# The adaLN modulation of a two-layer encoder: 16 blocks as products on TensorE ahead of the first norm, 32 behind retention and the second layer's 48 in the MLP, as row sums over transposed weights

## What is computed

```python
mod = jax.nn.silu(c) @ w_ada + b_ada            # (1024) @ (1024, 6144), for 2 vectors c
sh1, sc1, g1, sh2, sc2, g2 = jnp.split(mod[:, None, :], 6, axis=-1)
h = _rmsnorm(x, norm1_g) * (1.0 + sc1) + sh1
mix, new_state = _token_mixers(h, ...)
x = x + g1 * (mix @ w_out)
h = _rmsnorm(x, norm2_g) * (1.0 + sc2) + sh2
x = x + g2 * (jnp.square(jax.nn.relu(h @ w_up)) @ w_down)
```

## Time and profile before

| | |
|---|---|
| median of 3 runs | 3626.52 us (3621.28 to 3632.74) |
| profiled execution | 3623.91 us |
| its span | 3622.1 us |
| PE busy | 3361.5 us, 93% |
| DVE busy | 1731.1 us, 48% |
| ACT busy | 950.7 us, 26% |
| POOL busy | 871.6 us, 24% |
| weight units, 512 KB each | 212, median 3.7 us from issue to landing |
| adaLN units, 384 KB each | 128, median 3.8 us |

### The profile page before, as it was taken

The page is one execution under the profiler, slowest core; times in us unless marked ns, Lnnn a source line. Parts: engine busy times, 40 slices in busy tenths (PEclk is TensorE's granted clock), DMA queues, the critical chain, the costliest instruction groups (busy, mean ns, idle before and its releaser), DMA issues.

```text
span 3622.1 us, 50742 instructions
## 1 busy us (share of the span) xinstructions
PE 3361.5 (93%) x19632; PEld 3031.9 (84%) x19632; DVE 1731.1 (48%) x2991; ACT 950.7 (26%) x1697; POOL 871.6 (24%) x478
## 2 busy tenths in 40 slices
PE   3499999899998999999998999998999999999998
PEld 2497889766777999999998878985667899999998
DVE  6833522365448554445565352325643833333335
ACT  2013111266343111111122231116644411111112
POOL 0121222222122232223223112231212222233231
PEclk7599999999998999999999999999999999999999
DMA  6521136723411222222212112565232111111111
GB/s 220 161 65 38 49 102 185 222 66 70 89 37 63 71 71 71 80 70 73 81 53 80 43 30 82 164 210 141 61 70 52 41 41 42 46 46 41 46 47 66
DMA packets 139878, 297.54 MB, mean 82 GB/s; under 512 B 52940, under 2 KB 73748, under 8 KB 138816
## 3 DMA queue, kind: packets, MB, share of 16 engines
q1 hardware_dynamic: 96912, 217.82, 21.4%
q10 hardware_dynamic: 42800, 77.46, 6.6%
HBM read 228.45 MB, written 53.56 MB: 78 GB/s over the span
## 4 chain that ended last, share of the span: by engine, by line
PE 74%; DVE 11%; issue 3%; ACTq 3%; DMA 3%; PEld 3%; ACT 2%; SPq 1%; POOL 0%; DVEq 0%; POOLq 0%; PEldq 0%
PE ps L1253 19%; PE ps L1228 13%; PE ps L1169 9%; PE ps L901 6%; PE ps L956 4%; DVE ada_acc L1792 4%; PE ps L1146 3%; PE ps L1039 3%; PE ps L1082 2%; PE ps L1102 2%; PE ps L883 2%; PE ps L736 2%; PE ps L925 1%; DVE tn L1862 1%; DVE act_lo L2221 1%
## 5 line engine op out<-in xcount | busy, mean ns | idle before, releaser
L658 POOL CAST w_hi<-raw 128x1024 fp32r<-128x1024 f32 x212 | 231.8, 1093 | 2261.0 <-PEq L1259 534.8
L2039 DVE SCALAR_TENSOR_TENSOR x<-ps,mod,x 128x352 f32<-128x352 f32 (+2 forms) x768 | 352.7, 489 | 516.5 <-PE ps L1253 426.5
L661 POOL TENSOR_TENSOR w_lo<-raw,w_hi 128x1024 fp32r<-128x1024 f32 x212 | 522.0, 2462 | 36.7 <-POOL w_hi L658 36.7
L1253 PE MATMUL ps<-act_hi,w_hi 128*128 128x352 f32 x1536 | 507.9, 331 | 19.3 <-DVE act_lo L2221 12.7
L1253 PE MATMUL ps<-act_lo,w_hi 128*128 128x352 f32 x1536 | 503.9, 328 | 0.0
L1253 PE MATMUL ps<-act_hi,w_lo 128*128 128x352 f32 x1536 | 501.6, 327 | 0.0
L1228 PE MATMUL ps<-h_hi,w_hi 128*128 128x352 f32 x1344 | 434.8, 324 | 10.1 <-DVE x L2039 7.7
L1228 PE MATMUL ps<-h_hi,w_lo 128*128 128x352 f32 x1344 | 430.9, 321 | 0.0
L1228 PE MATMUL ps<-h_lo,w_hi 128*128 128x352 f32 x1344 | 430.8, 321 | 0.0
L1707 ACT ACTIVATE relu_b<-ps,consts 128x352 f32<-128x352 f32 x192 | 106.3, 554 | 1181.9 <-PE ps L1228 1156.8
L1169 PE MATMUL ps<-pT,vb 128*128 128x512 f32 (+5 forms) x1080 | 398.4, 459 | 9.2 <-ACT pT L1621 9.2
(11 more groups left out here) (214 smaller groups left out, 6087.6 us busy)
## 6 DMA issues: line engine op xcount, KB each, us to landing
raw<-in_w SPq DMA_DIRECT2D x212, 512.0 KB, 3.7
ada_w<-in_w_ada SPq DMA_DIRECT2D x128, 384.0 KB, 3.8
kb<-scr_k SPq DMA_DIRECT2D x36, 328.0 KB
kb<-scr_k SPq DMA_DIRECT2D x60, 164.0 KB
qb<-scr_q SPq DMA_DIRECT2D x36, 264.0 KB
qb<-scr_q SPq DMA_DIRECT2D x60, 132.0 KB
scr_k<-hi ACTq DMA_DIRECT2D x12, 656.0 KB, 4.0
scr_k<-lo ACTq DMA_DIRECT2D x12, 656.0 KB, 5.8
```

Of the source, the lines that this page charges most:

```text
L658: pool.tensor_copy(hi, raw[:, uc % 2, 0:width]).then_inc(pool_hi, 1)
L661: pool.tensor_tensor(lo, raw[:, uc % 2, 0:width], hi.bitcast(F32), ALU.subtract).then_inc(w_ready, 1)
L1253: last = mm(ps[:, i % 6, 0:GW], w[:, k * 256 + o * 128:k * 256 + o * 128 + 128], (act_lo if low else act_hi)[:, k * T + g * GW:k * T + (g ...
L2039: last = v.scalar_tensor_tensor(xs, ps[:, bank, a - g * GW:b - g * GW], gs, xs, ALU.mult, ALU.add)
```

## The change

Layer 1's blocks 0 to 15 are made by PE directly, `ada_first`. Their weights lie in SBUF as they are, 128 x (8 x 2048), 8.4 MB in four loads on SP, borrowed from the region of h_hi and h_lo. For each row block k and each block b one matmul takes the 128x128 weights as its fixed operand and cond, 128x2, as the moving one: 128 matmuls, N=2, accumulated in bank 7. The squares of the first norm are now added up by DVE as for the other norms (`add`), so PE has one statistics matmul per group in place of eight, and these stand behind `ada_first` in PE's list, all through one bank. x is loaded in four parts.

All other blocks go by another form. Their weights come transposed: 128 partitions are 128 outputs, with 1024 inputs along the row. cond is spread over all partitions through a DRAM buffer (`cond_all`). One `tensor_tensor_reduce` on DVE multiplies a block by it and sums the row, so no sum over partitions and no PE is needed. There are two such operations per block, one for either vector.

Layer 1's blocks 16 to 47 are done behind retention's items 9 to 32 (`ADA_ITEMS`), one or two per item. Their weights are loaded on ACT's queue into five buffers in the region of x, which nobody reads then; the next load is issued one item later. Behind the last, x is loaded again, and DVE waits for it ahead of the first residual. Layer 2's blocks are done in the MLP of layer 1, six per chunk, behind the evictions of up's items 4 to 9, from three buffers; SP loads them behind raw units 0, 1, 2, 5, 6 and 7 (`ADA_LOADS`).

```diff
-ADA_AT, ADA_SUM_AT, ADA_KEPT_AT = 4, 8, 11
+ADA_AT, ADA_KEPT_AT = 4, 2
+X_PARTS = 4
+ADA_LOADS = [0, 1, 2, 5, 6, 7]
...
+ADA_ITEMS = [9 + n * 24 // ADA_BACK for n in range(ADA_BACK)]
...
+            def ada_first():
+
+                for k in range(KB):
+                    if k % 2 == 0:
+                        pe.wait_ge(nat_in[k // 2], 16)
+                    for b in range(ADA_FIRST):
+                        last = mm(ps[:, 7, 2 * b:2 * b + 2], ada_nat[:, k, b * 128:(b + 1) * 128], cond[:, k, :],
+                                  start=(k == 0 and b == 0), stop=(k == KB - 1), skip_group_check=True)
                 last.then_inc(mod_ps, 1)
...
-                    if li + 1 < L and i == ADA_SUM_AT:
-                        ada_sum(li + 1, f, 0)
...
-            first_stats()
-            for f in range(ADA_CHUNKS):
-                ada_sum(0, f, f % 2)
+            ada_first()
+            for g in range(GROUPS):
+                stat(0, g)
...
+                    for n in range(ADA_BACK):
+                        if li == 0 and ADA_ITEMS[n] == y - 1:
+                            if n + ADA_SLOTS[0] < ADA_BACK:
+                                act.wait_ge(ada_done, 2 * n + 2)
+                                ada_load(n + ADA_SLOTS[0])
+                            elif n == ADA_BACK - 1:
+                                act.wait_ge(ada_done, 2 * ADA_BACK)
+                                act.dma_start(x[:], I["x"]).then_inc(x_back, 16)
...
+            def ada_block(li, n, z, loaded, dst):
+
+                dve.wait_ge(ada_in[z], loaded)
                 for q in range(2):
...
+                    dve.wait_ge(ada_done, n + q)
+                    v.tensor_tensor_reduce(ada_out[li][:], ada_w[li][:, z, :], cond_all[li][:, q, :], 1.0, 0.0, ALU.mult, ALU.add,
+                                           dst[:, q:q + 1]).then_inc(ada_done, 1)
...
                     evict(n, i, first)
-                    if li + 1 < L and i >= ADA_AT:
-                        ada_unit(li + 1, f, i - ADA_AT, 0)
+                    if li + 1 < L and ADA_AT <= i < ADA_AT + ADA_PER:
+                        ada_next(f, i - ADA_AT)
```

More of the change, by code:

```diff
@@ L190 @@
 SWEEP_GAPS = [3, 7, 11, 15, 19, 23]
+ADA_ITEMS = [9 + n * 24 // ADA_BACK for n in range(ADA_BACK)]
+ADA_LOADED = [len(range(z, ADA_BACK, ADA_SLOTS[0])) for z in range(ADA_SLOTS[0])]
 def ret_gaps():
@@ L618, in attend @@
                 raw_load(li * NU + 41, 1)
+            nat_load(0)
+            raw_load(0, 0)
+            nat_load(1)
+            raw_load(1, 1)
+            nat_load(2)
+            sp.wait_ge(cond_ready, 2)
+            sp.dma_start(scr_cond.rearrange("q (p k) -> p q k", p=128), cond_q[:]).then_inc(cond_out, 16)
+            nat_load(3)
             for li in range(L):
-                for u in range(OUT1_BASE):
+                for u in range(0 if li else 2, OUT1_BASE):
                     raw_load(li * NU + u, u % 2)
@@ L1316, in done @@
                 act.drain().then_inc(act_done, 1)
-            def first_squares():
-                act.wait_ge(x_in, 16)
-                for m in range(24):
-                    g, k = divmod(m, KB)
-                    if m >= SQS:
-                        act.wait_ge(sq_used, m - SQS + 1)
-                    A(sq[:, m % SQS, :], x[:, k * T + g * GW:k * T + (g + 1) * GW], ACT.Square, bias=zero).then_inc(sq_ready, 1)
             def square(c, i, kept, count):
                 b, g = OUT_ORDER[i]
-                act.wait_ge(kept, count + i + 1)
+                if c:
+                    act.wait_ge(kept, count + i + 1)
+                else:
+                    act.wait_ge(x_in[b * X_PARTS // KB], 16)
                 if i >= 3 + SQS:
@@ L1736, in _ @@
             A(lam_e[:], lam_s[:], ACT.Exp, bias=zero).then_inc(lam_exp, 1)
-            first_squares()
+            for i in range(24):
+                square(0, i, None, 0)
             for g in range(GROUPS):
@@ L1830, in prologue @@
                 lambdas()
-                for f in range(ADA_CHUNKS):
-                    for u in range(KB):
-                        if f >= 2 and u == 0:
-                            dve.wait_ge(mod_ps, f - 1)
-                        ada_unit(0, f, u, f % 2)
-                        if u == 2 and f:
-                            ada_kept(0, f - 1)
-                ada_kept(0, ADA_CHUNKS - 1)
-                scales(0)
+                for i in range(24):
+                    add(0, i)
+                ada_first()
                 done()
@@ L2021, in pairs @@
                         ret_gap(li, jj, gap)
+                    for n in range(ADA_BACK):
+                        if li == 0 and ADA_ITEMS[n] == y:
+                            ada_behind(n)
+                if li == 0:
+                    dve.wait_ge(x_back, 16)
                 for i in range(24):
```

162 lines of the change are left out of this document (93 added, 69 removed).

## The result

The changed kernel takes 3648.13 us (median of 5, 3646.98 to 3658.01), the kernel before 3626.52 (3621.28 to 3632.74). The ratio is 1.006, with a 95% interval of 1.0049 to 1.0072: the change costs 0.6%. The profiled execution took 3646.98 us, its span is 3645.2, 23.1 more than before.

The account below looks back on a forecast made before the run. PE was taken to bound the kernel (74% of the chain), so changes pay where PE waits less. Terms −82 + 11 + 1 − 3 + 69 = −4 gave 3619.9, with 2.6 added about 3623 us; range 3583 to 3670.

Parts of the forecast that it names:

- PE starts at 15.6: Prologue: cond is ready about 1 us behind its exponential, so PE begins the 128 small matmuls at 15.6 us.
- −82: Prologue: steady product at 82.9 us against 166.2, PE at half clock; −82 us (−78 to −86).
- I take +11: Retention of layer 1: added DVE operations make PE wait; +11 us out of 4 to 25.
- The loop: Seven later MLP chunks: late weight blocks lengthen each from 98.86 to 108.7 us; +69 us (63 to 78).
- Block 5's 12.8 behind D0: MLP loop chunk: the sixth block's late load delays item 10's eviction to D0 + 12.8; PE stands 10.8 us.
- D0: The first matmul of down in an MLP chunk, from which the forecast counts the late load's steps.
- block 4's 2.4: MLP loop chunk: the fifth block's load, pair and item 9's eviction make the start of down 2.4 us late.
- First chunk −3: First MLP chunk: loses its sum, gets six pairs of 2.58 where it had 8 of 1.95; −3 us (−8 to +2).
- x read again +1: End of retention: second read of x lands at 378 against first residual at 377; +1 us (0 to 3).
- (b): Rival, MLP loop: the sixth block isn't on the path, chunk 97.5 us, loop gives −10, total 3544; chance 0.06.
- (c): Rival, DVE: accumulating multiply over two SBUF tensors runs at half the plain product's pace; total about 3718; chance 0.12.
- (a): Rival, prologue: first products at full clock, weights' arrival at 45 us decides, gain 25 larger, total 3598; chance 0.10.

Follow-up runs that it names:

- the first kernel with wide products: Changed kernel with constants and cond loaded first, and the 16 blocks made with cond as fixed operand and weights moving, 512 columns: 3623.5 us, ratio 0.9993.

## Why the prediction was wrong

The form of the answer was right: a large gain at the start, given back in seven pieces by one late load. Two costs were taken too small, and since gain and loss nearly cancel, they decided the sign. In the profiled executions −4 was forecast and +23.1 measured. Of these 27 us the start has 11.8, retention 10.8, the loop 3.8 and the first chunk 3.9; the stretch with x read again has −2.3, and attention and layer 2, to which no term was given, +1.7 and −2.6.

- **"PE starts at 15.6"** was wrong by 12.9 us, and so −82 became −70. The step that failed is the time until cond is ready, in which nothing was put for the landing of cond and for slower issues. I had priced the x issues that stand ahead of the exponential, at 0.5 each, and asked whether the 8.4 MB would hide behind the products. I didn't ask what they do to whoever shares the DMA engines. SP's list of before, with 384 KB loads through four buffers, never had so much in flight, so ACT's issues of 0.45 and cond's landing in 4.0 us in that trace were prices under other conditions; here an issue took up to 4.42 and the landing 16.1. The other parts of the term held: 54.74 for 54.8 (256 × 0.213 is 54.5), 12.6 for 12.5. Holding SP's loads and moving the exponential ahead brought the steady product to 83.4.
- **"I take +11"** for retention measured 21.8, within its 4 to 25, and the choice in the range was the error; the step that failed is the slack that I gave DVE's small operations against PE's next item. "Most of DVE's gap work has slack against PE's next item" was argued from DVE's mean load. PE stood 12 us more than before. The sum of DVE's work was mis-sized too: 64 operations at 1.43 with POOL beside them are 91, and 96 with their accumulator reads, not 83, and the four blocks on three short items met three splits right there. I counted 4 us of backlog from the mean and none from these splits, though the earlier trace rows showed a two-input operation at 2.68 beside a split. The Trainium skill ("SBUF — State Buffer", "SBUF: two separate sides") calls the port pair of DVE and GpSimd an exclusive lock and not a split of bandwidth. The trace agrees: the operation that starts at 140.35 ends at 143.65, and POOL's subtraction ends at 142.57; 1.23 behind that is 143.80, 0.15 from it. And I priced PE's standing only, not the slow matmuls behind it: the clock of the second window is 0.91 for 0.99, and that was worth 9 us.
- **The loop** held: +69 forecast, 72.8 measured, 10.4 a chunk for 9.8. Block 5's 12.8 behind D0 came out to the tenth; block 4's 2.4 measured 2.9 (POOL's cast at D0 comes 13.5 us behind the one before it, with both blocks in down 10.6). One detail was wrong: D0 comes behind a wait of 2.8 us itself, so item 0 runs slowly and takes 3.6 us in place of 1.95; the standstill is 9.2 and not 10.8, and there are two slow restarts and not one. The sum is nearly the same.
- **First chunk −3** came out at +0.9, within its bounds. **x read again +1** (0 to 3): the stretch that holds it came out at −1.3, below its bounds, but DVE did stand 0.69 us for x. The run with ACT two items later shows how near that was to its edge.
- **Rivals.** (b) fell: the load was on the path, and moving it gave 82 us. (c) fell: the accumulating product takes 1.23 us for 1024, the pace of the plain one; the halving that the Trainium skill ("Vector Engine (DVE) Microarchitecture Reference", "7. Points that are easy to get wrong") states for the S2S2D2_STT form doesn't appear with this operation; whether it is of that form, no run shows. (a) fell: the narrow products took 0.214 us each, to the end. Its 45 us for the weights' arrival had no working: 14 MB at 439 GB/s are 32 us.

One miss of judgement is in no term. The costs of which the trace showed nothing, ACT's shared queue and the meetings in retention, were taken at nothing and near the low end, though DMA traffic and DVE's work only grew there. A more even choice would have put more on slower than on faster; 0.23 and 0.38 were the wrong way round.

## What to carry to other kernels

Work for an idle engine is free only if its inputs are there when its turn comes: for each piece, follow its load back to the semaphore that lets it be issued, and see whether the engine that gives this semaphore waits for something queued behind that piece. Here a block moved two items later turned 3648 us into 3566 with no other difference. When a change puts large transfers at the head of one queue, price the small ones of all other queues again, and issue those first that start the critical engine.

## What the runs showed of the hardware

- With 7 MB issued by SP in the first 3.3 us, the issue of a small DMA on ACT's queue took up to 4.42 us instead of 0.45, and the issues up to x ended at 26.7 instead of 12.3. cond, 8 KB, landed 16.1 us behind the start of its issue instead of 4.0. In the first kernel with wide products a table of 1 KB needed 24 us. Neither shows in the bandwidth, which was good: 420 GB/s from 5 to 20 us.
- The megabytes alone don't set an issue's time. With cond first, twelve tables were issued on ACT's queue from 7.3 us on, beside SP's 8.4 MB, at 0.33 to 0.96 us each; the four parts of x behind them then took 2.1 to 4.1 each. What an issue waits for, no run separates.
- A product with accumulator on DVE over two SBUF tensors, 128x1024, takes 1.23 us alone and 3.30 when it starts within POOL's subtraction, which grows from 2.4 to 3.2 when it starts within such a product.
- A standstill of PE of 2.8 us was followed by slow matmuls: 0.29 us from start to start where it had been 0.16, for ten of them from 1430.39 on, at a granted clock of 0.50, then 0.22. So short waits cost more than they last. In retention 12 us of standing came with 9 of slow work, behind the late read of x 4.2 with 7.6.
- Products with N=2 and 128x128 weights took 0.214 us per instruction for 256 in a row, the pace of the sums at a clock of 0.50, with PE busy throughout. The same sums with the weights moving ran at 0.86 us per instruction from 15.8 us and at 0.43 from 20 us on, 29.8 us in all.
